# Second mixer on one Trainium2 core: differential output ahead of a weight unit, and first-layer weight units ahead of the norms

## Chip, cores and metric
The kernel runs on one core of a Trainium2 chip. The metric is the device time of one execution in microseconds; lower is better.

## The reference
Two blocks follow each other on an activation of 256 tokens by 1024 features, in float32, each with two layers. The second block's layer is, cut to what matters here:

```python
h = rms_norm_2(x, attn_norm)
proj = h @ w_in                     # 1024 x 5444
aq, ak, av, iq, ik, iw, bq, bk, bv, gates = split_cols(proj)
...                                 # head norms and rotary embedding
ya = sparse_attention(aq, ak, av, iq, ik, iw, k_sel)     # 64 best keys by index scores
yb = diff_attention(bq, bk, bv, lam)                     # p0 - lam * p1
yb = rms_norm_2(yb, b_subln) * (1.0 - lam_init)
g_a, g_b = sigmoid(gates + gate_bias)
x = x + (g_a * (ya @ w_up_a) + g_b * (yb @ w_up_b)) @ w_out
x = x + (silu(gate) * up) @ w_ffn_out                    # of rms_norm_2(x, ffn_norm)
```
The first block has other mixers and two feed-forward parts per layer, and ends with a norm, so that the second block's first layer works on a normed activation: its norm comes out of two sums of squares.

## The kernel before
Every float32 matmul by a weight is done as three: the weight is split into a high part (rounded) and a low part (the rest), and so is the activation, and high by high, high by low and low by high are added up (`three`, L1953). Weights come in units of 128 x 2048 elements, 1 MB, through four buffers. SP loads a unit into `raw`; ScalarE makes the high part (`split`, L709, busy at L717), VectorE the low part (`split`, L1215, busy at L1222), and TensorE consumes it (`split_ready`, L1959). Each engine has its own program, an order written out by hand, and they meet at semaphores. A unit can be split once the unit four before it is used.

A layer of the second mixer projects in 11 column tiles of two units each (`full_k`, L1979): positions 0 to 15 of a tile, one position being the three matmuls of one 128-row slice of the weights. Positions 0 to 3 and 8 to 11 are the first 128 tokens, the others the second. When a tile's first half is done (position 11, semaphore `tile_half`), the copy or gate of that half may begin. Beside the positions, functions `beside_bk` (tile 2) to `beside_g3` (tile 10) put the attention's small work: turns (transposes) of rotated heads (`turn`), index scores, then for each pair of heads scores (`pair_qk`), the turn of the probabilities (`pair_turn`), and the product with the values (`diff_pv`, `sparse_pv`). Pairs 0 to 3 belong to the differential attention, 4 to 7 to the sparse one.

What touches the change:

- **Start of a layer.** ScalarE turns the transposed activation into high parts with the gain (`stage`, L743), VectorE into low parts (L1245). Squares are summed on ScalarE (`square`, L719; in the first layer also `square_scaled`, L997), VectorE makes the mean (`norm`, or `two_norms`, L1232), ScalarE the root. ScalarE's copy of tile 0 (`evac(0)`, L1031) needs it. GpSimd then rotates the index heads and their key (`rotate2`, from L649), scales, copies (L686) and signals `rot_ready`, for which `rotated(0)` in `beside_bk` waits on TensorE, ahead of `turn((0, 1))`. Turned items are copied by ScalarE (`item(0)`) and VectorE (`item(1)`, L1355); item 5 is VectorE's last, and the first scores (`pair_qk(0)`, L2490) in tile 5 wait for it.
- **End of the projections.** At position 8 of tile 10 TensorE turns the differential output (L1965), ScalarE copies high parts (`diff_hi`, L1104), VectorE makes the low parts (`diff_lo`, L1796). At position 12 comes `pair_turn(7)` (L2505), which waits for `diff_lo`, since both use the same banks. VectorE's `gate(10, 0)` (L1703) needs tile 10's `tile_half`. `probs_turned(7)` copies the turned pair 7 on ScalarE (one half) and VectorE (the other, L1785); `sparse_pv(7)` (L2532) waits for both. It stands behind the first position of the up-projection, whose units are P2_UP to P2_UP + 3.

Of the kernel before, what the change touches and what calls it, by code (L numbers as in the profile page):

```python
# [56 lines left out]
P2_UP = P2_WIN + 2 * len(WIN2)  # L57
# [5 lines left out]
GAIN_FFN1, GAIN_MIX, GAIN_FFN2, GAIN_ATTN, GAIN_FFN, GAIN_FINAL = (2 * KC * k for k in range(6))  # L63
# [37 lines left out]
def stream1(l):  # L101
    return Stream(l * U1)
# [6 lines left out]
def build(nc, I, out):  # L109
    L = DEPTH  # L110
    with ExitStack() as ctx:
# [278 lines left out]
        PARTS = ((0, 0), (0, 1), (1, 0), (1, 1))  # L390
# [317 lines left out]
        def _(act):  # L708
            def split(st, p, it=0, m=None, c=4):  # L709
                s = st.slot(p)  # L710
                act.wait_ge(loaded[s], st.loads(p, it))

                act.wait_ge(units_used, st.freed(p, it))
                src, dst = raw[:, s, :], w_hi[:, s, :]
                if m is not None:
                    src, dst = (a.rearrange("p (c n) -> p c n", c=c)[:, :, 0:m] for a in (src, dst))
                nc.scalar.activation(dst, src, ACT.Copy).then_inc(units_hi, 1)  # L717

            def square(X, i, dump=xn, col=0):  # L719

                act.wait_ge(x_ready, X * 2 + (i + 1))
                nc.scalar.activation(dump[:, i, :], x[:, i, :], ACT.Square, accum_out=ss[:, col + i:col + i + 1])
# [20 lines left out]
            def stage(S, gain=None, parts=PARTS, first=0, banks=STAGE_BANKS):  # L743
                for n, (i, g) in enumerate(parts, first):
                    act.wait_ge(stage_T, S + (n + 1))
                    bank = ps[:, banks[2 * i + g], :].rearrange("p (c t) -> p c t", c=4)
                    tok = slice(P * i, P * i + P)
                    if gain is None:
                        o = nc.scalar.activation(aT_hi[:, 4 * g:4 * g + 4, tok], bank, ACT.Copy)
                    else:  # L750
                        for c in range(4):
                            o = nc.scalar.activation(aT_hi[:, 4 * g + c, tok], bank[:, c], ACT.Copy,
                                                     scale=gain_cols[:, gain + 4 * g + c:gain + 4 * g + c + 1])
                    o.then_inc(stage_hi, 1)
# [75 lines left out]
            for l in range(L):  # L830
                st = stream1(l)
# [37 lines left out]
                def exps(k):  # L869

                    for e in range(2):
                        act.wait_ge(pair_masked, (J + k) * 4 + (2 * e + 2))
                        for i, (c, n) in enumerate(((0, P), (P, 2 * P))):
                            nc.scalar.activation(pair_p[:, k % 2, e, c:c + n], pair_p[:, k % 2, e, c:c + n], ACT.Exp,
                                                 bias=pair_max[:, k % 2, e, i:i + 1], scale=-1.0,
                                                 accum_out=pair_sums[:, k % 2, e, i:i + 1])
                        nc.scalar.drain()
                        act.sem_inc(pair_exp, 1)
# [111 lines left out]
            for l in range(L):  # L990
                st = stream2(l)
                B = l * STAGES2 + STAGES1 * L
                N, W, T = l * 2 + 6, l * 11, l * TJ2 + TJ1 * L
                J, O = l * PAIRS2 + PAIRS1 * L, l * 2 + 4 * L
                if l == 0:

                    def square_scaled(i):  # L997
                        act.wait_ge(final_scaled, i + 1)
                        nc.scalar.drain()
                        nc.scalar.activation(junk[:, i, :], xn[:, i, :], ACT.Square, accum_out=ss[:, i:i + 1])  # L1000

                    junk = att[:, 0:2 * DM].rearrange("p (i n) -> p i n", i=2)
                    stage(B, GAIN_ATTN, PARTS[:2])
                    square(6, 0, junk, 2)
                    square_scaled(0)
                    stage(B, GAIN_ATTN, PARTS[2:], first=2)
                    split(st, 2)
                    square(6, 1, junk, 2)
                    square_scaled(1)
                    squared()  # L1010
                    root(N, 4)
                else:
                    stage(B, GAIN_ATTN + l * KC, PARTS[:2])
                    square(l * 2 + 7, 0)
                    split(st, 2)
                    stage(B, GAIN_ATTN + l * KC, PARTS[2:], first=2)
                    square(l * 2 + 7, 1)
                    squared()
                    root(N)
# [80 lines left out]
                def diff_hi():  # L1100

                    for i in range(2):
                        act.wait_ge(stage_T, B + (5 + i))
                        nc.scalar.activation(yb_hi[:, :, P * i:P * i + P],  # L1104
                                             ps[:, 6 + i, :].rearrange("p (c t) -> p c t", c=4), ACT.Copy)\
                            .then_inc(stage_hi, 1)
# [3 lines left out]
                        .then_inc(gates2_ready, 1)  # L1110

                evac(0)
                split(st, 3)
                head_squares(0)
                win_split(2, 0)
                head_roots(0)
# [68 lines left out]
                split(st, P2_UP)  # L1185
                probs_turned(6)
                exps(7)
                split(st, P2_UP + 1)
                diff_hi()
                split(st, P2_UP + 2)  # L1190
                probs_turned(7)
                act.wait_ge(tile_done, W + 9)
# [19 lines left out]
        def _(dve):  # L1212
            V = nc.vector

            def split(st, p, it=0, m=None, c=4):  # L1215
                s = st.slot(p)

                dve.wait_ge(units_hi, st.index(p, it) + 1)
                a, h, o = raw[:, s, :], w_hi[:, s, :].bitcast(F32), w_lo[:, s, :]
                if m is not None:  # L1220
                    a, h, o = (v.rearrange("p (c n) -> p c n", c=c)[:, :, 0:m] for v in (a, h, o))
                V.tensor_tensor(o, a, h, ALU.subtract).then_inc(units_split, 1)  # L1222
# [9 lines left out]
            def two_norms(N):  # L1232

                dve.wait_ge(squares, N + 1)
                V.tensor_scalar(ss[:, 2:4], ss[:, 2:4], 1.0 / DM, EPS, ALU.mult, ALU.add)
                V.tensor_scalar(ss[:, 0:2], ss[:, 0:2], 1.0 / DM, None, ALU.mult)
                V.drain()
                V.scalar_tensor_tensor(ss[:, 0:2], ss[:, 2:4], EPS, ss[:, 0:2], ALU.mult, ALU.add).then_inc(mean_sq, 1)  # L1240
                dve.wait_ge(roots, N + 1)
                V.reciprocal(rstd[:, 0:4], rstd[:, 0:4]).then_inc(rstd_ready, 1)
                V.drain()
# [172 lines left out]
            for l in range(L):  # L1416
                st = stream1(l)
# [248 lines left out]
            for l in range(L):  # L1666
                st = stream2(l)
                B = l * STAGES2 + STAGES1 * L
                N = l * 2 + 6
                if l == 0:  # L1670
                    stage(B, GAIN_ATTN, PARTS[2:], first=2)
                    split(st, 2)
                    two_norms(N)
                    split(st, 3)
                else:
                    stage(B, GAIN_ATTN + l * KC, PARTS[2:], first=2)
                    split(st, 2)
                    norm(N)
                    split(st, 3)
# [16 lines left out]
                def gate(n, i):  # L1696

                    c0, m = WIN2[n]
                    if i == 0:
                        dve.wait_ge(tile_half, l * 11 + (12 + n + 1))  # L1700
                    else:
                        dve.wait_ge(units_used, st.used(P2_WIN + 2 * n + 1))
                    V.scalar_tensor_tensor(proj2[:, i, c0:c0 + m], ps[:, BANK2[n][i], :], rstd[:, i:i + 1],  # L1703
                                           proj2[:, 1, c0:c0 + m], ALU.mult, ALU.add)\
                        .then_inc(tile_done if i else gate_first, 1)
                    V.drain()  # L1706
# [206 lines left out]
                probs_turned(6)  # L1913
                masked(7)
                probs(7)
                split(st, P2_UP + 1)
                diff_lo()
                gate(10, 0)
                split(st, P2_UP + 2)
                probs_turned(7)  # L1920
                gate(10, 1)
# [28 lines left out]
        def _(pe):  # L1950
# [18 lines left out]
            def stage(src, ready, n, i, banks=STAGE_BANKS):  # L1969

                pe.wait_ge(ready, n * 2 + (i + 1))
                turned(src, i, 0, banks)
                turned(src, i, 1, banks)
# [180 lines left out]
            for l in range(L):  # L2154
                st = stream1(l)
# [283 lines left out]
            for l in range(L):  # L2439
                st = stream2(l)  # L2440
                T, W, A, D = l * TJ2 + TJ1 * L, l * 11, l * 5 + 10, l * 5 + 12
                B, J, O = l * STAGES2 + STAGES1 * L, l * PAIRS2 + PAIRS1 * L, l * 2 + 4 * L
# [92 lines left out]
                    o.then_inc(pair_out, 1)  # L2535

                def beside_bk(at):
                    if at == 8:
                        rotated(0)
                        turn((0, 1))  # L2540
                    if at == 14:
                        copied(1, 1)
                        index_scores(0)

# [96 lines left out]
                first = second_half(x, x_ready, 6 if l == 0 else l * 2 + 7)  # L2641
# [107 lines left out]
```

## Time and profile before

| | |
|---|---|
| median of 3 runs | 1790.18 us (1790.01 to 1791.67) |
| profiled execution | 1789.88 us |
| its span in the profile | 1788.2 us |
| TensorE busy | 1774.5 us, 99% |
| VectorE busy | 1231.3 us, 69% |
| ScalarE busy | 987.8 us, 55% |
| GpSimd busy | 225.8 us, 13% |
| granted TensorE clock | 1.00 |
| HBM read | 313.94 MB, 176 GB/s |

PE is TensorE, PEld its weight loads, DVE VectorE, ACT ScalarE, POOL GpSimd. Busy time counts an instruction from its start to its modelled end, and TensorE's overlap: matmuls of 512 columns last 0.39 us each but follow one another every 0.227 us. Times of a timeline are counted from the start of the span.

### The profile page before, as it was taken

The numbers are of one execution on the slowest core, as the hardware profiler recorded it, in microseconds if no ns is written. First come the engines' busy times: TensorE is split into PE (matmuls) and PEld (weight loads), VectorE is DVE, ScalarE is ACT, GpSimd is POOL, SyncE is SP. The second block draws the span as 40 slices with busy tenths as digits, with TensorE's granted clock in tenths as the row PEclk, the third lists the DMA queues.
The fourth block names the chain that finished last, engine by engine and source line by source line (L and its number), as shares of the span: only waits on it lengthen the run. The fifth ranks groups of instructions, "written<-read, shape, count | busy, mean of one in ns | idle before, by whom it ended". The sixth has DMA issues, their size and how long they took to land.

```text
span 1788.2 us, 25450 instructions
## 1 busy us (share of the span) xinstructions
PE 1774.5 (99%) x9448; PEld 1479.0 (83%) x9448; DVE 1231.3 (69%) x1753; ACT 987.8 (55%) x1333; POOL 225.8 (13%) x255
## 2 busy tenths in 40 slices
PE   9999999999999999999999999999999999999999
PEld 8888877888888888877888877778888877788887
DVE  6775667677557755767676479966775599867763
ACT  6555585555445554666555376555554466645551
POOL 0000121000000000320000096200001383100000
PEclk9999999999999999999999999999999999999999
DMA  8656472555546564544565564545656544545551
GB/s 266 222 195 204 138 208 72 187 188 188 210 145 195 193 226 143 190 118 141 189 197 201 168 205 128 177 130 186 196 194 212 164 166 142 188 157 175 191 204 74
DMA packets 221517, 316.26 MB, mean 177 GB/s; under 512 B 14168, under 2 KB 162288, under 8 KB 221168
## 3 DMA queue, kind: packets, MB, share of 16 engines
q1 hardware_dynamic: 221392, 315.02, 53.9%
q8 instruction: 57, 0.93, 0.2%
q14 instruction: 36, 0.29, 0.0%
q10 hardware_dynamic: 32, 0.01, 0.0%
HBM read 313.94 MB, written 1.05 MB: 176 GB/s over the span
## 4 chain that ended last, share of the span: by engine, by line
PE 84%; DVE 10%; DVEq 3%; ACT 2%; issue 1%; ACTq 0%; POOLq 0%
PE ps L2091 25%; PE ps L1955 14%; PE ps L1957 13%; PE ps L1956 13%; PE ps L2092 13%; DVE w_lo L1222 3%; PE ps L1965 1%; PE ps L2179 1%; PE ps L2206 1%; PE ps L2194 1%; DVEq L1706 1%; ACT w_hi L717 1%; DVEq L1742 1%; DVE score L1731 1%; DVE att L1755 1%
## 5 line engine op out<-in xcount | busy, mean ns | idle before, releaser
L1222 DVE TENSOR_TENSOR w_lo<-raw,w_hi 128x2048 fp32r<-128x2048 f32 (+2 forms) x296 | 674.7, 2302 | 200.8 <-ACT w_hi L717 199.1
L2091 PE MATMUL ps<-aT,w_hi 128*128 128x512 f32 x1920 | 667.7, 392 | 0.0
L717 ACT ACTIVATE w_hi<-raw 128x2048 fp32r<-128x2048 f32 (+2 forms) x296 | 551.6, 1892 | 159.0 <-PE ps L1957 155.8
L2092 PE MATMUL ps<-aT,w_lo 128*128 128x256 f32 x1920 | 536.9, 280 | 0.0
L2091 PEld LDWEIGHTS ps<-aT,w_hi 128*128 128x128 f32 x1920 | 359.4, 187 | 80.4 <-issue 0.3
L2092 PEld LDWEIGHTS ps<-aT,w_lo 128*128 128x128 f32 x1920 | 362.5, 189 | 0.2
L1955 PE MATMUL ps<-w_hi,aT 128*128 128x512 f32 (+2 forms) x768 | 309.3, 403 | 4.3 <-DVE w_lo L1222 2.8
L1957 PE MATMUL ps<-w_hi,aT 128*128 128x512 f32 (+2 forms) x768 | 295.1, 384 | 0.0
L1956 PE MATMUL ps<-w_lo,aT 128*128 128x512 f32 (+2 forms) x768 | 294.3, 383 | 0.0
L1955 PE MATMUL ps<-w_hi,gT_hi 128*128 128x512 f32 x528 | 206.0, 390 | 0.0
L1957 PE MATMUL ps<-w_hi,gT_lo 128*128 128x512 f32 x528 | 205.6, 389 | 0.0
L1956 PE MATMUL ps<-w_lo,gT_hi 128*128 128x512 f32 x528 | 205.5, 389 | 0.0
L1955 PEld LDWEIGHTS ps<-w_hi,aT 128*128 128x128 f32 x768 | 144.3, 188 | 46.1 <-issue 16.7
L1957 PEld LDWEIGHTS ps<-w_hi,aT 128*128 128x128 f32 x768 | 144.2, 188 | 29.2
L1956 PEld LDWEIGHTS ps<-w_lo,aT 128*128 128x128 f32 x768 | 144.6, 188 | 22.9
L766 ACT ACTIVATE att<-ps 128x512 f32<-128x512 f32 x60 | 35.8, 597 | 162.2 <-PE ps L2092 162.2
L1957 PEld LDWEIGHTS ps<-w_hi,gT_lo 128*128 128x128 f32 x528 | 99.1, 188 | 20.7
L1956 PEld LDWEIGHTS ps<-w_lo,gT_hi 128*128 128x128 f32 x528 | 99.2, 188 | 20.4
L1955 PEld LDWEIGHTS ps<-w_hi,gT_hi 128*128 128x128 f32 x528 | 99.1, 188 | 20.4
L1313 DVE TENSOR_TENSOR att<-ps,att 128x512 f32<-128x512 f32 x60 | 41.5, 692 | 78.6 <-ACT att L771 78.6
L768 ACT ACTIVATE att<-att 128x512 f32<-128x512 f32 x60 | 37.9, 632 | 104.3 <-DVE att L1311 104.3
L618 POOL COPY tt<-proj 128x512 f32<-128x512 f32 x4 | 4.1, 1050 | 635.1 <-DVE proj L1453 635.1
(289 smaller groups left out, 1704.4 us busy)
## 6 DMA issues: line engine op xcount, KB each, us to landing
raw<-in_w_in SPq DMA_DIRECT2D x120, 512.0 KB, 4.5
raw<-in_w_ffn_down SPq DMA_DIRECT2D x88, 512.0 KB, 4.4
raw<-in_w_ffn_in SPq DMA_DIRECT2D x88, 512.0 KB, 5.0
raw<-in_w_ffn_gate SPq DMA_DIRECT2D x86, 512.0 KB, 4.2
raw<-in_w_ffn_up SPq DMA_DIRECT2D x86, 512.0 KB, 5.2
raw<-in_w_ffn_out SPq DMA_DIRECT2D x44, 512.0 KB, 4.8
raw<-in_w_out SPq DMA_DIRECT2D x32, 512.0 KB, 4.7
raw<-in_w_ck SPq DMA_DIRECT2D x8, 512.0 KB, 3.9
```

What stands on the lines that cost most here:

```text
L717: nc.scalar.activation(dst, src, ACT.Copy).then_inc(units_hi, 1)
L766: nc.scalar.activation(sil[:, b % 2], ps[:, bg:bg + 2, SEQ:2 * SEQ], ACT.Copy).then_inc(gate_lo, 1)
L768: nc.scalar.activation(sil[:, b % 2], sil[:, b % 2], ACT.Silu).then_inc(silu_done, 1)
L1222: V.tensor_tensor(o, a, h, ALU.subtract).then_inc(units_split, 1)
L1313: V.tensor_tensor(gg[:, b % 2], ps[:, bu:bu + 2, 0:SEQ], gg[:, b % 2], ALU.add)
L1706: V.drain()
L1731: V.scalar_tensor_tensor(score[:, c:c + n], relu[:, h % 2, c:c + n], iw[:, i, h:h + 1], (causal if h == 0 else score)[:, c:c + n], ALU.mul ...
L1955: M(o, ah, wh, start=start, stop=False)
L1956: M(o, ah, wl, start=False, stop=False)
L1957: return M(o, al, wh, start=False, stop=stop)
L2091: M(o, wh, aT[:, :, k, :], start=k == 0, stop=False, skip_group_check=True)
L2092: r = M(o[:, 0], wl, aT_hi[:, k, :], start=False, stop=k == KC - 1, skip_group_check=True)
```

## The change
Four orders change, and no instruction is added or removed.

- First layer: ScalarE splits unit 2 ahead of `stage` of the second 128 tokens and unit 3 right behind it, both ahead of `square_scaled(0)` and the squares that follow; its split of unit 3 behind `evac(0)` stays in the second layer alone. VectorE splits unit 3 ahead of `two_norms`.
- Both layers: `diff_hi` stands ahead of the split of unit P2_UP + 1 on ScalarE, and on VectorE that split stands behind `diff_lo` and `gate(10, 0)`.
- Both layers: in tile 2, `turn((0, 1))` goes from position 8 to 11, `index_scores(0)` from 14 to 15.

```diff
@@ ScalarE, first layer of the second mixer
                     square(6, 0, junk, 2)
+                    split(st, 2)
+                    stage(B, GAIN_ATTN, PARTS[2:], first=2)
+                    split(st, 3)
                     square_scaled(0)
-                    stage(B, GAIN_ATTN, PARTS[2:], first=2)
-                    split(st, 2)
                     square(6, 1, junk, 2)
@@
                 evac(0)
-                split(st, 3)
+                if l > 0:
+                    split(st, 3)
                 head_squares(0)
@@ ScalarE, both layers
                 exps(7)
+                diff_hi()
                 split(st, P2_UP + 1)
-                diff_hi()
                 split(st, P2_UP + 2)
@@ VectorE, first layer
                     split(st, 2)
+                    split(st, 3)
                     two_norms(N)
-                    split(st, 3)
@@ VectorE, both layers
                 probs(7)
-                split(st, P2_UP + 1)
                 diff_lo()
                 gate(10, 0)
+                split(st, P2_UP + 1)
                 split(st, P2_UP + 2)
                 probs_turned(7)
@@ TensorE, both layers
                 def beside_bk(at):
-                    if at == 8:
+                    if at == 11:
                         rotated(0)
                         turn((0, 1))
-                    if at == 14:
+                    if at == 15:
                         copied(1, 1)
                         index_scores(0)
```

## Rows read from the trace of the kernel before

**Rows 1.** The page's busy times: busy us, share of the span, instructions.
```profile
PE 1774.5 (99%) x9448; PEld 1479.0 (83%) x9448; DVE 1231.3 (69%) x1753; ACT 987.8 (55%) x1333; POOL 225.8 (13%) x255
```

**Rows 2.** TensorE's waits: total us, times, longest.
```profile
PE ps L1955 <- DVE w_lo L1222: 2.8, 4, 0.8
PE ps L2505 <- DVE yb_lo L1796: 2.0, 2, 1.1
```

**Rows 3.** TensorE's timeline, first layer, tiles 1 and 2: start, duration, [idle before].
```profile
1031.86 0.50 PE L1955 MATMUL ps<-w_hi,aT 128*128 128x512 f32 x1 [0.35 <-DVE w_lo L1222]
...
1038.36 0.50 PE L1955 MATMUL ps<-w_hi,aT 128*128 128x512 f32 x1 [0.73 <-DVE w_lo L1222]
...
1043.94 0.39 PE L1955 MATMUL ps<-w_hi,aT 128*128 128x512 f32 x1
```

**Rows 4.** ScalarE's and VectorE's timelines, start of the first layer.
```profile
1023.17 1.06 ACT L1000 ACTIVATE att<-xn 128x1024 f32<-128x1024 f32 x1
...
1025.29 2.17 ACT L752 ACTIVATE aT<-ps,gain_cols 128x128 fp32r<-128x128 f32 x8 [0.97 <-PE ps L1965]
...
1026.47 2.16 DVE L1255 SCALAR_TENSOR_TENSOR aT<-ps,gain_cols,aT 128x128 fp32r<-128x128 f32 x8 [0.60 <-ACT aT L752]
...
1029.30 2.50 DVE L1222 TENSOR_TENSOR w_lo<-raw,w_hi 128x2048 fp32r<-128x2048 f32 x1 [0.68 <-ACT w_hi L717]
...
1032.80 0.95 ACT L1031 ACTIVATE proj<-ps,rstd 128x324 f32<-128x324 f32 x2 [0.24 <-DVE rstd L1242]
```

**Rows 5.** Timelines of GpSimd and TensorE's weight loads up to the first turns, first layer.
```profile
1036.11 2.78 POOL L656 TENSOR_TENSOR proj<-proj,cs 128x256 f32<-128x256 f32 x1
...
1050.04 0.31 PEld L2137 LDWEIGHTS ps<-ident,proj 128*128 128x128 f32 x3 [0.24 <-POOLq L687]
```

**Rows 6.** Windows: us, busy per engine (instructions), clock, DMA; then VectorE's timeline there.
```profile
1043.90:1082.20 38.30, 38.30 (x186) 30.41 (x184) 32.24 (x32) 22.64 (x27) 36.21 (x27) 1.00 0.66 219
...
1050.95 0.43 DVE L1355 TENSOR_SCALAR tt<-ps 128x256 f32<-128x256 f32 x1 [1.94 <-PE ps L2137]
...
1054.31 3.18 DVE L1222 TENSOR_TENSOR w_lo<-raw,w_hi 128x2048 fp32r<-128x2048 f32 x1 [0.18 <-ACT w_hi L717]
```

**Rows 7.** Timelines of VectorE and TensorE at the first scores, first layer.
```profile
1081.46 0.68 DVE L1355 TENSOR_SCALAR tt<-ps 128x512 f32<-128x512 f32 x1
...
1082.24 0.93 PE L2490 MATMUL ps<-tt 64*128 64x128 f32 x8
```

**Rows 8.** The same places in the second layer: item 1, first scores.
```profile
1431.33 0.42 DVE L1355 TENSOR_SCALAR tt<-ps 128x256 f32<-128x256 f32 x1 [3.44 <-PE ps L2137]
...
1462.92 0.93 PE L2490 MATMUL ps<-tt 64*128 64x128 f32 x8 [0.16 <-issue]
```

**Rows 9.** Timelines of TensorE, ScalarE and VectorE around pair 7, first layer.
```profile
1164.87 1.03 PE L1965 MATMUL ps<-ident,xn 128*128 128x128 f32 x8
1165.73 1.07 ACT L1104 ACTIVATE yb_hi<-ps 128x512 fp32r<-128x512 f32 x2
1165.86 2.29 DVE L1222 TENSOR_TENSOR w_lo<-raw,w_hi 128x2048 fp32r<-128x2048 f32 x1 [0.79 <-ACT w_hi L717]
...
1167.80 0.39 PE L1955 MATMUL ps<-w_hi,aT 128*128 128x512 f32 x1
1168.06 1.28 DVE L1796 TENSOR_TENSOR yb_lo<-ps,yb_hi 128x512 fp32r<-128x512 f32 x2
1169.26 0.74 DVE L1703 SCALAR_TENSOR_TENSOR proj<-ps,rstd,proj 128x512 f32<-128x512 f32 x1
1169.49 0.85 PE L2505 MATMUL ps<-ident,att 128*128 128x128 f32 x6 [0.85 <-DVE yb_lo L1796]
...
1172.31 0.55 DVE L1785 COPY xn<-ps 128x384 f32<-128x384 f32 x1
...
1173.07 0.87 PE L2532 MATMUL ps<-xn,proj 128*64 128x256 f32 x8
```

**Rows 10.** TensorE's timeline at pair 7, second layer.
```profile
1550.45 0.84 PE L2505 MATMUL ps<-ident,att 128*128 128x128 f32 x6 [1.14 <-DVE yb_lo L1796]
```

## Prediction
> **What bounds the kernel now.** The profiled execution took 1789.88 us (span 1788.2, 1.68 around it), 0.30 under the median of 1790.18; the sum is made against 1789.88. About 0.2% (3.6 us) is what a measurement of this kernel can tell from no change. I read the page's busy shares first: TensorE is busy 99% of the span [rows 1], so only the 13.7 us in which it isn't can be gained. The waits of TensorE come next, for who ends these gaps: VectorE's weight splits and its low part of the differential output lead [rows 2]. Then the timelines around each moved line. Three things are to be seen there. First, both units of projection tile 1 come late in the first layer of the second mixer [rows 3]. Second, between 1043.9 and 1082.2 TensorE never rests, yet VectorE's queue is full as well, 32.24 of 38.30 us with GpSimd at 36.21 [rows 6]; its last link, the copy of item 5, ends at 1082.14, 0.1 before TensorE's first scores of the pair loop at 1082.24 [rows 7]. Third, the turn of pair 7 waits 0.85 and 1.14 us for the low part [rows 9, 10].
>
> **The start of the first layer.** Tile 1's first unit waits for a split that VectorE began at 1029.30, 0.68 idle, because ScalarE's half stood behind `stage` [rows 4]. Moved ahead, ScalarE's half fits where `square_scaled(0)` stood, from 1023.17 for 1.9 us to 1025.1, before `stage` begins at 1025.29: nothing is pushed. VectorE's stage ends at 1028.63, its split (2.50) at 1031.1; TensorE is free at about 1031.3, since its wait is 0.35 and the refill of its pipeline some 0.15 more. Unit 3 follows on VectorE at 1031.1 and is there at 1033.6, against a need at 1036.8: the wait of 0.73 goes, with its refill [rows 3]. TensorE's second half of tile 1, unwaited, took 5.58 and its first 6.50 [rows 3], so 0.9. Together **1.5 to 1.65 us, taken 1.6**, at the start of tile 2.
>
> The norms pay for it. VectorE's split ended at 1031.8 and the scaled copy (`evac(0)`) began at 1032.80: a chain of 1.0 [rows 4]. Behind both splits it starts at 1033.6, so the copy at 1034.6, 1.8 later. ScalarE's squares don't decide: its stage ends at 1027.5, unit 3's split (1.9) at 1029.4, and three squares of about 1.2 at 1033.0. Who waits: GpSimd's rotation (the copy feeds it), which in turn releases the first turns. SP's loads into the two buffers go out sooner, not later; none of these rows waits for a DMA.
>
> **The first turns, from position 8 to 11.** In the profile TensorE took them at 1050.04 to 1050.06 as GpSimd let them go [rows 5]. Three positions are 9 matmuls of 0.227 (a position is 0.68: eight of them are the 5.58 of a unit in rows 3, less the refill), 2.04 us. In the first layer TensorE comes there at 1050.06 - 1.6 + 2.04 = 1050.5. GpSimd starts 1.8 later, but of its 16.3 us from the copy's end (1033.75) to 1050.04 some are not work: one operation took 2.78 beside a split, against a mean of 1.34 over 27 [rows 5, 6], so up to 2 us each are waiting, and VectorE's splits (which stood behind the late unit 3) now come up to 2 us sooner and block one operation fewer. I get 1050.4, bounds 1049.9 (all the delay is made up) and 1051.8 (none). **The turns are 0.4 later** (bounds 0 and 1.9). In the second layer nothing is gained ahead, so they are **2.04 later**.
>
> That matters since ScalarE's item 0, its head squares, VectorE's sums and then the split of unit 7 queue behind the turns: VectorE idled 1.94 and 3.44 us for them [rows 6, 8], and from 1052.5 to item 5 it doesn't idle for TensorE again. Item 5 lets the scores go at 1082.24 and, in the second layer, 1462.92 (0.16 idle, refill more) [rows 7, 8]. What the queue loses up to there TensorE loses, whatever it had won: in the first layer the 1.6 are gone and 0.4 stands as a loss. In the second it would be 2.04. The unit split just behind the turns took 3.18 against 2.29 where GpSimd rests [rows 6, 9]; with GpSimd 2 us further ahead one of them falls in VectorE's idle time. I take **1.8 us** (bounds 0.9 and 2.1). Index scores at 15 instead of 14: 0.68 later at most, behind a queue that is later anyway, so nothing.
>
> The Trainium skill, SBUF — State Buffer (Reading the diagram), says that VectorE with two SBUF inputs and a reading GpSimd operation exclude each other for a whole instruction. The 2.78 and the 3.18 of this trace agree. Where the rule speaks for a smaller loss is a rival below.
>
> **The differential output ahead of unit P2_UP+1.** Before: VectorE splits from 1165.86, low parts 1168.06 to 1169.34, TensorE turns pair 7 at 1169.49; free it was at 1167.80 + 0.68 = 1168.48 [rows 9]. After: TensorE's transposes begin at 1164.87, the first four are done about 0.6 later, ScalarE's high parts (1.07 for both) end at 1166.6, VectorE's low parts at 1167.5. The wait goes, 1.0 us. But what is late next? `gate(10, 0)` now follows at once and needs tile 10's first half, whose last matmul ends at about 1168.65: VectorE, which used to split in this time, idles 1.2 us. Then 0.74 for the gate, 2.29 twice for the units UP+1 and UP+2, 0.55 for the copy of the turned pair 7 [rows 9]: 1168.7 + 0.1 + 0.74 + 4.5 + 0.5 = 1174.5. Before, that copy ended at 1172.86, and `sparse_pv(7)` began at 1173.07, just behind. It waits for it; now it begins at 1174.7, though TensorE is there at 1172.05. A wait of 2.6 stands in place of one of 1.0: **+1.6 us** (bounds 1.3 and 1.8). ScalarE ends its part of the turned pair at 1166.6 + 2 x 1.9 + 0.5 = 1170.9 and isn't the one waited for. Unit UP+1, split by 1171.8, is needed after `sparse_pv(7)` and the rest of unit UP, 21 matmuls of 0.227, at 1179 or later: hidden. SP's load into the buffer that this split frees goes out 3.7 us later (1171.8 for 1168.1); three units of 5.5 us still lie ahead of its use, so it costs nothing unless a load takes over 10 us. In the second layer the old wait was 1.14 instead of 0.85 [rows 10], so 0.3 less is lost: **+1.3** (1.0 and 1.6).
>
> **Sum.** 0.4 + 1.8 + 1.6 + 1.3 = 5.1; 1789.88 + 5.1 = **1795.0**. Ends: 0 + 0.9 + 1.3 + 1.0 = 3.2 and 1.9 + 2.1 + 1.8 + 1.6 = 7.4, so 1793.1 to 1797.3.
>
> **Rivals.**
> - *VectorE runs free of GpSimd behind the later turns* (not slower by more than 0.2%). The split behind them paid 0.9 over the free price [rows 6, 9]; if it and the next one run free, VectorE gets 1.8 back per layer: 0.4 - 1.8 = -1.4 and 2.0 - 1.8 = 0.2 at the first scores, with the ends' 2.9: +1.7, 1791.6. It decides once some 1.5 us in all are regained, which brings the sum of 5.1 to 3.6. For it: GpSimd gets 2 us of VectorE's idle time in the second layer. Against: it is busy 36.21 of 38.30 us and always has the next operation pending [rows 6]. By the rule of the Trainium skill, SBUF — State Buffer (Reading the diagram), this is the outcome if GpSimd runs out of work. Chance 0.12.
> - *GpSimd late at the turns.* One more operation blocked by a split, 2 us: turns at 1051.8 or beyond, 1.5 more: 6.6, 1796.5. Chance 0.12.
> - *Only the turn of pair 7 gains.* If something else than the copy held `sparse_pv(7)`, the ends bring -2.3, and with +2.2 ahead of them nothing is left: 1789.8. Against it stands the copy's end 0.2 before that matmul, and a plain queue. Chance 0.12.
> - *Every removed wait is gained* (faster): -1.6 - 1.0 - 1.3 = -3.9, 1786.0. It decides if VectorE's queue has 2 us to spare ahead of 1082 and 2.6 at pair 7; it shows no idle time there. Chance 0.06.
>
> **How the numbers follow.** My forecast has 0.58, and some 0.08 of it lies under 3.6 us. Slower 0.50 + 0.12 = 0.62 (rounded); within 0.2%: 0.08 + 0.12 + 0.12 and half of the last, 0.35; faster 0.03. The range leaves out the last two rivals and reaches from the first (1791.6, less 0.6 for runs and bounds) to the upper bound: 1791.0 to 1797.5.
>
> **What would show it.** The w_lo waits of tile 1 and the yb_lo waits gone; `evac(0)` of the first layer near 1034.6; turns at 1050.5 in the first layer and 2.04 later from the start of the layer in the second; item 5 on VectorE at 1081.9 in the first layer and, counted from the start of its layer, 1.8 later in the second, with a wait of TensorE of 2 us at or just behind the first scores in both; a new wait of 2.6 at `sparse_pv(7)` for the copy at L1785. If that wait is absent, the forecast is wrong by 3 to 5 us; if VectorE's item 5 isn't later, by about 2.

## The result, and the profile after

The changed kernel took 1795.46 us in the median of 10 runs (1793.33 to 1798.27), beside 1790.18 us of the kernel before (10 runs, 1789.75 to 1792.10) on the same chip: a ratio of 1.0025 [1.0017, 1.0033], 5.3 us slower. The profiled execution took 1795.33 us, with a span of 1793.6 and a granted clock of 1.00.

The page's span and busy times; they differ from [rows 1] by at most 0.7 us, so no engine has more work:

```profile
span 1793.6 us, 25450 instructions
PE 1774.9 (99%) x9448; PEld 1479.5 (82%) x9448; DVE 1232.0 (69%) x1753; ACT 987.8 (55%) x1333; POOL 226.3 (13%) x255
```

TensorE's waits after (total us, times, longest):

```profile
PE ps L2534 <- DVE xn L1787: 3.8, 2, 1.9
PE ps L2479 <- ACT xn L1066: 2.4, 2, 1.2
PE ps L1957 <- DVE w_lo L1224: 1.7, 2, 0.9
...
PE ps L2139 <- POOLq L666: 0.9, 2, 0.5
```

Against [rows 2], the two waits of tile 1's units and both waits of `pair_turn(7)` for `yb_lo` are gone. In their place stand two of 1.9 at `sparse_pv(7)` (L2534) for VectorE's copy of the turned pair, two of 1.2 at the second group of index scores (L2479), and two of 0.5 at the second turns.

TensorE's timeline where each second-mixer layer begins, before and then after. All times below are counted from these starts:

```profile
1022.90 0.31 PE L1955 MATMUL ps<-w_hi,aT 128*128 128x324 f32 x1
...
1404.73 0.31 PE L1955 MATMUL ps<-w_hi,aT 128*128 128x324 f32 x1
```
```profile
1024.90 0.31 PE L1957 MATMUL ps<-w_hi,aT 128*128 128x324 f32 x1
...
1407.75 0.31 PE L1957 MATMUL ps<-w_hi,aT 128*128 128x324 f32 x1
```

The mixer starts 2.0 us later after, though nothing ahead of it was changed; more on this under "What the hardware showed". From there:

| us from the layer's start | first turns | first scores | `pair_turn(7)` | `sparse_pv(7)` |
|---|---|---|---|---|
| first layer, before | 27.16 | 59.34 | 146.59 | 150.17 |
| first layer, after | 27.56 | 59.49 | 145.72 | 151.19 |
| second layer, before | 25.73 | 58.19 | 145.72 | 149.30 |
| second layer, after | 27.77 | 60.02 | 146.29 | 151.75 |

The first scores are 0.15 and 1.83 later, the stretch from there to `sparse_pv(7)` is 0.87 and 0.62 longer: 3.5 us in all. With the 2.0 of the start that is the span's difference, 1793.6 - 1788.2 = 5.4.

Start of the first layer after, timelines of VectorE and ScalarE, then of GpSimd, TensorE and VectorE up to the first scores:

```profile
1030.55 4.73 DVE L1224 TENSOR_TENSOR w_lo<-raw,w_hi 128x2048 fp32r<-128x2048 f32 x2
...
1036.29 0.95 ACT L1032 ACTIVATE proj<-ps,rstd 128x324 f32<-128x324 f32 x2 [0.25 <-DVE rstd L1244]
...
1051.38 0.40 POOL L686 COPY att<-proj 128x256 f32<-128x256 f32 x1
...
1052.46 0.60 PE L2139 MATMUL ps<-ident,proj 128*128 128x128 f32 x4
...
1053.31 0.42 DVE L1357 TENSOR_SCALAR tt<-ps 128x256 f32<-128x256 f32 x1 [4.75 <-PE ps L2139]
...
1060.32 0.93 PE L2479 MATMUL ps<-tt 64*128 64x128 f32 x8 [1.16 <-ACT xn L1066]
1066.69 1.09 PE L2139 MATMUL ps<-ident,proj 128*128 128x128 f32 x8 [0.45 <-POOLq L666]
...
1084.39 0.93 PE L2492 MATMUL ps<-tt 64*128 64x128 f32 x8
```

VectorE makes both units' low parts in one go, and the scaled copy of tile 0 starts 11.39 from the layer's start, 1.49 later than in [rows 4] (9.90). GpSimd's copy ends at 1051.78 (1051.38 + 0.40), and TensorE takes the turns at 1052.46 without a wait. VectorE idles 4.75 us ahead of item 1 where it had idled 1.94 [rows 6]. TensorE then stops twice within 14 us of the turns. In the second layer:

```profile
1435.52 0.60 PE L2139 MATMUL ps<-ident,proj 128*128 128x128 f32 x4
...
1436.38 0.42 DVE L1357 TENSOR_SCALAR tt<-ps 128x256 f32<-128x256 f32 x1 [5.46 <-PE ps L2139]
...
1467.77 0.93 PE L2492 MATMUL ps<-tt 64*128 64x128 f32 x8 [0.16 <-issue]
```

Here VectorE's idle time grew from 3.44 to 5.46 [rows 8], the 2.04 of three positions.

What leads from the first turns to TensorE's next stops can be read from GpSimd's rotation of the next heads. Its operation at L655 waits for ScalarE's squares of these heads (L1042, L1043 after), which stand in ScalarE's queue behind item 0, the copy of the first turns. That operation in the two layers, before and then after:

```profile
1052.80 1.29 POOL L655 TENSOR_TENSOR proj<-proj,rg 128x512 f32<-128x512 f32 x1
...
1433.17 1.30 POOL L655 TENSOR_TENSOR proj<-proj,rg 128x512 f32<-128x512 f32 x1
```
```profile
1054.91 1.29 POOL L655 TENSOR_TENSOR proj<-proj,rg 128x512 f32<-128x512 f32 x1 [0.42 <-ACT proj L1043]
...
1437.98 1.30 POOL L655 TENSOR_TENSOR proj<-proj,rg 128x512 f32<-128x512 f32 x1 [1.95 <-ACT proj L1043]
```

From the layer's start it begins at 29.90 and 28.44 before, at 30.01 and 30.23 after: 0.11 and 1.79 later. From there to TensorE's second turns 11.7 to 11.8 us pass in all four layers, and these turns come at 41.65 and 40.18 before, at 41.79 and 42.03 after: 0.14 and 1.85 later, as the first scores are. VectorE's item 5 ends 0.1 us ahead of the first scores in all four, and TensorE's idle time there (none, and 0.16) is the old one.

Pair 7 in the first layer after, to be laid beside [rows 9]:

```profile
1168.28 1.29 DVE L1798 TENSOR_TENSOR yb_lo<-ps,yb_hi 128x512 fp32r<-128x512 f32 x2 [1.05 <-ACT yb_hi L1105]
...
1169.94 0.39 PE L1957 MATMUL ps<-w_hi,aT 128*128 128x512 f32 x1
...
1170.14 0.75 DVE L1705 SCALAR_TENSOR_TENSOR proj<-ps,rstd,proj 128x512 f32<-128x512 f32 x1 [0.58 <-PE ps L1959]
1170.62 0.82 PE L2507 MATMUL ps<-ident,att 128*128 128x128 f32 x6
1170.98 4.50 DVE L1224 TENSOR_TENSOR w_lo<-raw,w_hi 128x2048 fp32r<-128x2048 f32 x2
1175.39 0.55 DVE L1787 COPY xn<-ps 128x384 f32<-128x384 f32 x1
1176.09 0.87 PE L2534 MATMUL ps<-xn,proj 128*64 128x256 f32 x8 [1.89 <-DVE xn L1787]
```

`pair_turn(7)` no longer waits. But two splits, 4.50 us, stand between the gate and the copy that `sparse_pv(7)` needs; before, one of them had already run.

### The profile page after: what moved, and what is told of

It reads as the page before. It is cut to its first block, busy times and chain, and to the rows that moved or that the text cites. A ratio compares the mean times of both kernels' runs of the same rounds, so it can differ in the third digit from the quotient of the medians.

```text
span 1793.6 us, 25450 instructions
## 1 busy us (share of the span) xinstructions
PE 1774.9 (99%) x9448; PEld 1479.5 (82%) x9448; DVE 1232.0 (69%) x1753; ACT 987.8 (55%) x1333; POOL 226.3 (13%) x255
## 4 chain that ended last, share of the span: by engine, by line
PE 87%; DVE 8%; DVEq 2%; ACT 1%; issue 1%; DMA 0%; ACTq 0%; POOL 0%; SPq 0%
PE ps L2093 25%; PE ps L1957 15%; PE ps L1959 14%; PE ps L1958 14%; PE ps L2094 13%; DVE w_lo L1224 2%; PE ps L1967 1%; PE ps L2208 1%; PE ps L2181 1%; PE ps L2196 1%; DVEq L1744 1%; DVE score L1746 1%; DVEq L1736 1%; DVE score L1733 1%; PE ps L2139 1%
```

## Experiments

The theory: turns at position 11 hold VectorE's and ScalarE's queues back by 1.8 us, which TensorE pays, in the first layer out of what the units ahead win; and at pair 7 the wait for `yb_lo` is traded for a longer one for the copy at L1787. The rivals: VectorE's queue is not what TensorE pays for, the moved units themselves cost something, or something other than the copy holds `sparse_pv(7)`. Edits below are to the kernel before unless said otherwise. One table for all. Two columns give by how much each layer's stretch from its start to `sparse_pv(7)` is longer than before's (150.17 and 149.30), in one profiled execution; then come the lowest of 10 to 12 runs less the lowest of the kernel before beside them, and the ratio of the runs with its interval.

| kernel | 1st layer | 2nd layer | sum | lowest run | ratio |
|---|---|---|---|---|---|
| the changed kernel | +1.02 | +2.45 | +3.5 | +3.6 | 1.0025 [1.0017, 1.0033] |
| e1, turns alone | +1.70 | +1.78 | +3.5 | +3.7 | 1.0019 [1.0010, 1.0027] |
| e2, pair 7 alone | +0.86 | +0.53 | +1.4 | +1.6 | 1.0010 [1.0002, 1.0019] |
| e3, first units alone | -0.18 | +0.04 | -0.1 | -0.1 | 0.9991 [0.9982, 0.9999] |
| e4, pair 7, copy first | +1.31 | -1.10 | | -1.7 | 0.9988 [0.9979, 0.9997] |
| e5, changed + copy first | -0.66 | +0.74 | +0.1 | -0.1 | 0.9996 [0.9987, 1.0005] |
| e6, changed, 2nd layer's turns at 8 | +0.93 | +0.61 | +1.5 | +1.6 | 1.0013 [1.0004, 1.0022] |
| e7, e3 and e4 together | -0.97 | -1.07 | -2.0 | -2.1 | 0.9993 [0.9984, 1.0002] |
| e7 again | -0.99 | -1.12 | -2.1 | -2.1 | 0.9986 [0.9977, 0.9995] |
| e8 | -0.85 | -0.94 | -1.8 | -1.8 | 0.9988 [0.9979, 0.9997] |
| e9 | -1.23 | -1.37 | -2.6 | -2.6 | 0.9985 [0.9976, 0.9994] |

The sum of the two stretches, from a single execution, agrees with the lowest run of each kernel to 0.2 us (e4's profile holds a disturbance, told there, and has no sum). So what these edits do lies in the two stretches. The medians scatter by 2 us around this, for two causes that stand under "What the hardware showed".

**e1: the later turns alone.**
```diff
                 def beside_bk(at):
-                    if at == 8:
+                    if at == 11:
                         rotated(0)
                         turn((0, 1))
-                    if at == 14:
+                    if at == 15:
```


> The kernel before with the one edit in beside_bk: first turns at position 11, first index scores at 15, both layers. My theory: VectorE's queue starts behind the turns and has no slack up to item 5, so TensorE loses what the turns lose less some 0.2: about 1.8 us in each layer, +3.6 in all, seen as item 5 and the first pair's scores 1.8 later, counted from the layer's start. Rival (VectorE makes it up, free of GpSimd): under 1 us in all. Second rival (later turns cost nothing by themselves, it was GpSimd's late start): 0.

Measured: median 1795.19 us, 1.0019 [1.0010, 1.0027]. The first scores come at 61.08 and 59.98, 1.74 and 1.79 later, and the rest is as before. TensorE's waits:

```profile
PE ps L1955 <- DVE w_lo L1222: 2.8, 4, 0.8
...
PE ps L2137 <- POOLq L666: 2.8, 2, 1.4
PE ps L2505 <- DVE yb_lo L1796: 2.0, 2, 1.2
```

The old waits of [rows 2] all stand; new is the wait of 1.4 in each layer at the second turns (`turn((2, 3))`, in tile 3) for GpSimd, plus one of 0.2 at the index scores. GpSimd's operation at L655, which ran without a wait before, here idles 1.88 us for ScalarE's squares in the first layer and 1.93 in the second. So later turns cost 1.8 us in each layer, and TensorE pays them at what ScalarE and GpSimd make for it, ahead of item 5. In the changed kernel's profile the same loss is split otherwise (1.2 at the index scores, 0.5 at the turns) and comes to the same; e5, whose orders are the changed kernel's up to pair 7, splits it as e1 does.

**e2: pair 7 alone.**
```diff
 ScalarE
+                diff_hi()
                 split(st, P2_UP + 1)
-                diff_hi()
 VectorE
-                split(st, P2_UP + 1)
                 diff_lo()
                 gate(10, 0)
+                split(st, P2_UP + 1)
                 split(st, P2_UP + 2)
                 probs_turned(7)
```


> The kernel before with diff_hi and diff_lo ahead of the split of unit P2_UP+1 on ScalarE and VectorE, as in the change, and nothing else. My theory: the waits of pair_turn(7) go (0.85 and 1.14), a wait of about 1.9 for VectorE's copy of the turned pair appears at sparse_pv(7) in both layers, net +0.9 and +0.6, +1.5 us. Rival (the wait's removal is the whole effect): -2.3 us. Rival (my first sum, a gate that waits 0.7 longer): +2.9.

Measured: median 1793.98 us, 1.0010 [1.0002, 1.0019]. Its wait in the first layer:

```profile
1175.73 0.87 PE L2532 MATMUL ps<-xn,proj 128*64 128x256 f32 x8 [1.89 <-DVE xn L1785]
```

`pair_turn(7)` comes 1.02 and 1.36 earlier, `sparse_pv(7)` 0.86 and 0.53 later: the changed kernel's two terms, without its other parts. The wait is the copy's, not something else's, and it is larger than the one removed.

**e3: the first layer's units alone.**
```diff
 ScalarE, first layer
+                    split(st, 2)
+                    stage(B, GAIN_ATTN, PARTS[2:], first=2)
+                    split(st, 3)
                     square_scaled(0)
-                    stage(B, GAIN_ATTN, PARTS[2:], first=2)
-                    split(st, 2)
...
-                split(st, 3)
+                if l > 0:
+                    split(st, 3)
 VectorE, first layer
                     split(st, 2)
+                    split(st, 3)
                     two_norms(N)
-                    split(st, 3)
```


> The kernel before with units 2 and 3 split ahead of the norms in the first layer, and the turns left at position 8, the pair 7 order left as it was. My theory: both waits of tile 1 go (0.35 and 0.73), TensorE comes to the turns 1.6 us earlier and waits there for GpSimd, which is ready at about the old time: a wait of 1.3 to 1.5 us at the turns, then everything as before: -0.2 us, between -0.4 and +0.3. Rival (the gained 1.6 us stay gained): -1.6.

Measured: median 1789.96 us, 0.9991 [0.9982, 0.9999]; the first scores are 0.16 earlier. Waits:

```profile
PE ps L1957 <- DVE w_lo L1224: 1.7, 2, 0.8
...
PE ps L2139 <- POOLq L687: 1.3, 1, 1.3
```

The interval lies under 1 because of the kernel before: 19 of its 35 runs beside e3 are above 1791 us, and one of e3's 11 (for the causes under "What the hardware showed"). The lowest runs and the stretches differ by 0.1. The waits at tile 1 go, as wanted, and one of 1.3 comes at the first turns, whose GpSimd work starts later. The units ahead are harmless and gain nothing by themselves: GpSimd, not the units, sets when the first turns can be. In the changed kernel this wait is absent because the turns have been moved behind it, and the queues pay.

**e4: pair 7, with the copy ahead of the second split.** ScalarE as in e2; VectorE:
```diff
-                split(st, P2_UP + 1)
                 diff_lo()
+                split(st, P2_UP + 1)
                 gate(10, 0)
-                split(st, P2_UP + 2)
                 probs_turned(7)
+                split(st, P2_UP + 2)
```


> The kernel before with diff_hi ahead of the split on ScalarE, and on VectorE the order diff_lo, split of P2_UP+1, gate(10, 0), copy of the turned pair 7, split of P2_UP+2. My theory: VectorE's copy is done at about 1171.1 in the time of before, before TensorE comes to sparse_pv(7) at 1172.05, so both waits are gone in both layers: -2.3 us. Rival (the copy isn't what sparse_pv(7) waits for in the changed kernel, or a later wait takes the gain): 0 or more.

Measured: median 1789.92 us, 0.9988 [0.9979, 0.9997]; the second layer's stretch is 1.10 shorter. In the first layer of the profiled execution VectorE's split for tile 1 took 4.44 us instead of 2.50 [rows 4]:

```profile
1029.43 4.44 DVE L1222 TENSOR_TENSOR w_lo<-raw,w_hi 128x2048 fp32r<-128x2048 f32 x1 [0.68 <-ACT w_hi L717]
...
1033.93 0.80 PE L1955 MATMUL ps<-w_hi,aT 128*128 128x512 f32 x1 [2.29 <-DVE w_lo L1222]
```

That is ahead of anything the kernel changes. From the first scores to `sparse_pv(7)`, behind it, 89.98 us stand against 90.83 before, 0.85 shorter. So most of the two old waits for `yb_lo` can be gained once only one split stands between the low part and the copy: e2 lost 1.4 us and e4 gains 2.0 (0.85 + 1.10) where 2.3 were expected, with a wait of 0.2 left at `sparse_pv(7)`. Against e2 two moves were made together: the split of P2_UP + 1 goes ahead of the gate as well. No run has them apart. By the changed kernel's durations the gate first, then one split and the copy would end at about 1173.7 (1170.14 + 0.75 + 2.29 + 0.55), ahead of 1174.20, when TensorE comes to `sparse_pv(7)`. By this estimate the copy's place ahead of the second split would be enough.

**e5: the changed kernel with that order on VectorE.**
```diff
                 diff_lo()
-                gate(10, 0)
                 split(st, P2_UP + 1)
-                split(st, P2_UP + 2)
+                gate(10, 0)
                 probs_turned(7)
+                split(st, P2_UP + 2)
```


> The changed kernel with VectorE's order at pair 7 mended: diff_lo, split of P2_UP+1, gate(10, 0), copy of the turned pair 7, split of P2_UP+2. My theory (sizes from the sections of the profiles so far): the layers cost +0.15 and +1.83 at the first scores and bring 0.9 and 1.1 at pair 7, so the profile stands within 0.3 us of the kernel before with no wait at sparse_pv(7). And the granted clock: I hold that its falls in the changed kernel come behind the waits of 1.9 us at sparse_pv(7), so without them no run should show a clock under 1.00 more often than runs of the kernel before do. Rival (the falls come from something else in the change): clocks of 0.999 and 0.998 in half of the runs, as in the changed kernel.

Measured: median 1789.80 us, 0.9996 [0.9987, 1.0005]. Pair 7 in the first layer:

```profile
1170.62 2.29 DVE L1224 TENSOR_TENSOR w_lo<-raw,w_hi 128x2048 fp32r<-128x2048 f32 x1 [1.00 <-ACT w_hi L717]
1172.84 0.74 DVE L1705 SCALAR_TENSOR_TENSOR proj<-ps,rstd,proj 128x512 f32<-128x512 f32 x1
1173.74 0.56 DVE L1787 COPY xn<-ps 128x384 f32<-128x384 f32 x1 [0.17 <-issue]
```

`sparse_pv(7)` waits 0.19 instead of 1.89, and 3.4 us of the changed kernel's 3.5 are back (1.02 + 0.66 and 2.45 - 0.74). What is left of the loss is the second layer's turns, hidden here by the two gains. On the clock: none of its 11 runs shows one under 1.00, against 3 of 33 of the kernel before beside it, so the rival (half of the runs) fails.

**e6: the changed kernel, in the second layer with the turns at 8 and 14.**
```diff
-                    if at == 11:
+                    if at == (11, 8)[l]:
...
-                    if at == 15:
+                    if at == (15, 14)[l]:
```


> The changed kernel with the first turns at position 8 and the index scores at 14 again in the second layer alone. My theory: the first scores of the second layer come 58.2 us after the layer's start instead of 60.0, 1.8 less for the whole kernel, so +1.65 against before in the profile; first layer unchanged at 59.5. Rival (VectorE's other work sets item 5, not the turns): no difference, +3.5.

Measured: median 1793.47 us, 1.0013 [1.0004, 1.0022]. The second layer's first scores come at 58.21, as before (58.19), and its stretch is longer by pair 7's 0.61 alone. The turns' 1.8 in the second layer is thus measured from both sides, by putting them in (e1) and by taking them out.

**e7: units ahead and copy first, turns left at 8** (e3 and e4 together).

> The kernel before with units 2 and 3 ahead of the norms in the first layer, turns at 8 in both layers, and at pair 7 the mended order (copy ahead of the split of P2_UP+2). My theory: -0.2 at the first scores of the first layer, 0 in the second, -0.9 and -1.1 at pair 7: -2.2 us, faster than both kernels. Rival (the parts aren't additive, e.g. a wait for a later up unit takes the gain): 0.

And for the second time:

> e7 unchanged, for a comparison on one chip with the version above: -2.1 us against before in the lowest run and in the sections of the profile. If its median again stands within 0.5 us of before while its lowest run is 2 us under it, the runs fall into two groups some 2 us apart that the change doesn't make.

Measured: median 1789.71 us, 0.9993 [0.9984, 1.0002], and, run again beside e9, 1787.94, 0.9986 [0.9977, 0.9995]. Both executions give the same stretches to 0.05 us. The second median doesn't stand within 0.5 us of before, but 2.3 under it (1790.26): 9 of the 11 runs were in the lower of two groups, where it had been 5 of 11. Of its waits, one of 1.3 stands at the first turns, as in e3. Parts that don't touch each other add up: -0.1 of e3 and -2.0 of e4, against -2.0 and -2.1 measured. It leaves the 1.3 at the first turns.

**e8: e5, with unit 7 split ahead of the turned items.** This asks whether VectorE's idle time ahead of the late turns can be used.
```diff
 ScalarE
                 evac(1)
+                win_split(3, 1)
                 item(0)
                 head_squares(1)
-                win_split(3, 1)
                 head_roots(1)
 VectorE
+                win_split(3, 1)
                 item(1)
                 head_sums(1)
-                win_split(3, 1)
                 head_scales(1)
```


> The changed kernel with the mended order at pair 7, and with the split of tile 3's second unit ahead of item 0 on ScalarE and of item 1 on VectorE, in both layers, so that it fills the time in which both wait for the later turns. My theory: VectorE's queue behind the turns is shorter by one split (2.3 to 3.2 us), so it isn't the bound at item 5; GpSimd's rotation is blocked by the split for up to 2 us, and TensorE waits for it at the turns by up to 2 us in the first layer and about 0 in the second. Net at the first scores: about -0.5 to +0.5 in the first layer, 0 to -0.5 in the second, then up to 1 us more per layer as the later waits for VectorE (0.3, 0.5, 0.8) shrink; with the pair 7 gain some -3 us. Rival (VectorE's queue isn't what binds at the first scores): item 5 comes no sooner than in the changed kernel, total near 0.

Measured: median 1788.20 us, 0.9988 [0.9979, 0.9997]. VectorE's timeline:

```profile
1058.34 2.72 DVE L1224 TENSOR_TENSOR w_lo<-raw,w_hi 128x2048 fp32r<-128x2048 f32 x1 [1.55 <-ACT w_hi L717]
1060.98 1.78 DVE L1733 SCALAR_TENSOR_TENSOR score<-xn,iw,causal 128x128 f32<-128x128 f32 x2
...
1081.76 0.68 DVE L1357 TENSOR_SCALAR tt<-ps 128x512 f32<-128x512 f32 x1
```

The second layer's first scores come at 58.36, 1.65 earlier than in e5 (60.01): the late turns cost almost nothing once work stands ahead of them. In the first layer they come only 0.13 earlier, since TensorE waits 1.3 at the first turns (28.96). In place of the full queue there is now an idle stretch of 1.55 for ScalarE's half of tile 4's first unit. In that stretch GpSimd's operation at L658 has no split beside it. Second layer, e5 and then e8:

```profile
1439.06 3.14 POOL L658 TENSOR_TENSOR proj<-proj 128x512 f32<-128x512 f32 x1
```
```profile
1437.36 1.28 POOL L658 TENSOR_TENSOR proj<-proj 128x512 f32<-128x512 f32 x1
```

The rotation starts no sooner (L655 at 30.48, in e5 at 30.24), but takes 1.86 less there, and the second turns come at 40.41 for 41.99, without the wait of 1.4 for GpSimd. VectorE's score operations are 1.65 sooner too, as expected; but the wait that TensorE lost was the one for GpSimd. The whole gain was 1.8 us where some 3 were expected.

**e9: e8, with ScalarE's split of that unit ahead of its roots.**
```diff
                 head_squares(1)
+                win_split(4, 0)
                 head_roots(1)
-                win_split(4, 0)
```


> As e8, and on ScalarE the split of tile 4's first unit ahead of the root of the second head norm, both layers: in e8 VectorE idled 1.55 us for that split, 3.3 us after the turns, which gave back what the moved unit 7 had won. My theory (VectorE's queue from the turns to the ninth tile is one chain, and TensorE's later waits of 0.3, 0.5, 0.3 and 0.8 us hang on it): item 5 comes about 1.8 us sooner than in e8 in both layers, the first scores 0.3 to 0.5 sooner, the later waits shrink, 3 us less than e8 in all, lowest run near 1785. Rival (the later waits hang on other work, or TensorE's own pace is the bound at the first scores and nothing behind it moves): 0 to -0.8 against e8.

Measured: median 1787.61 us, 0.9985 [0.9976, 0.9994].

```profile
1058.36 2.88 DVE L1224 TENSOR_TENSOR w_lo<-raw,w_hi 128x2048 fp32r<-128x2048 f32 x1
1061.16 2.81 DVE L1733 SCALAR_TENSOR_TENSOR score<-xn,iw,causal 128x128 f32<-128x128 f32 x2
...
1082.97 0.68 DVE L1357 TENSOR_SCALAR tt<-ps 128x512 f32<-128x512 f32 x1
```

The idle stretch is gone and VectorE's split begins 1.59 earlier from the layer's start (33.52 for 35.11; the starts are 1024.84 and 1023.23), but item 5 comes only 0.40 earlier. Of the 1.43 with which the next pair of operations starts ahead, 1.03 is lost in it (2.81 for 1.78). That is a miss: an idle gap in a queue is not worth its length here. The whole gain against e8 is 0.8 us in the stretches and in the lowest run, where 3 were expected; it is the rival's figure. e9 is the best of the kernels tried and beats both; against e7 in the same runs it is 0.3 us in the median and 0.5 in the stretches, too little to call.

## Why the prediction was right, and where not

The direction, and 1795.0 against a median of 1795.46, came out, though not by the sum's own terms: these were 5.1 and measured 3.5. That the total is so near is luck.

- **First scores, first layer:** 0.4 forecast, 0.15 measured. The turns came at 27.56, just 0.4 later than before. Right in that what tile 1 wins the first turns lose (e3); of the 0.4, GpSimd's rotation at L655 took over only 0.11. The scaled copy came 1.49 later and not 1.8.
- **First scores, second layer:** 1.8 forecast, 1.83 measured, 1.79 in e1, 1.8 in e6. The size was right, the path was not: I looked for a wait at or just behind the first scores, and in the first layer it stood 24 and 18 us ahead of them (1060.32 and 1066.69, against 1084.39), in the second 24 and 18 as well, at the index scores and the second turns. The second turns wait for GpSimd's rotation, and that for ScalarE's squares behind item 0; VectorE's sums aren't in this chain. The index scores wait for a copy of ScalarE, whose root before it had waited 0.86 for those sums. I followed VectorE's queue alone. That queue is late by as much (its score operations begin 38.19 us from the second layer's start, before 36.35), so what it would cost TensorE by itself isn't separated; but the wait ahead of the first scores didn't grow. And the 0.2 that I took off the three positions' 2.04 fits another cause: in the second layer before, the squares were done at 1432.86, 0.3 ahead of L655 (1433.17), and that slack is used up first.
- **Pair 7:** 1.6 and 1.3 forecast, 0.87 and 0.62 measured. This is the step that was mis-sized, by 0.7 in each layer: the start of `gate(10, 0)`, and with it the new wait at `sparse_pv(7)`. The mechanism held (e2 shows it alone, e4 and e5 undo it): the new wait was 1.89 and not 2.6. I let tile 10's first half end just before `pair_turn(7)`, at 1168.65 of before. But `tile_half` is signalled at position 11 and `pair_turn(7)` stands behind the matmuls of position 12, which [rows 9] show at 1167.80, a position before the turn. So the gate could begin 0.68 sooner: after, it starts 0.48 ahead of `pair_turn(7)` (1170.14, 1170.62). All that follows on VectorE (0.75, 4.50, 0.55) was as costed.
- **The rest,** 5.4 - 3.5 in the profiled execution, is the later start of the mixer (below). It is in the median too: the two middle runs, 1795.33 and 1795.60, show a clock of 1.00, and five others with falls of the clock reach up to 1798.27. No step forecast either, and by luck their size made up for the error at pair 7.

Of the rivals: "VectorE free of GpSimd" fails, the second layer loses 1.83 and not 0.2; "GpSimd late at the turns" fails, the turns came when forecast; "only the turn of pair 7 gains" fails at the copy's wait; "every removed wait is gained" fails too: with another order most of it is gained at pair 7 (e4), but at the start e3 gains 0.1.

## What to carry over

A removed wait is worth what the next thing in the same queue leaves of it. Ahead of moving an operation, write down who waits for the *end* of the queue behind it; moving a weight split of 2.3 us behind a small urgent copy instead of ahead of it turned, together with the gate's move behind the first split, a loss of 1.4 us into a gain of 2.0. Follow every queue that the moved operation releases: here the price of the later turns came through ScalarE's squares and GpSimd's rotation, and not at the end of VectorE's queue. And where one engine lies on the path 99% of the time, compare sections of the trace from a common matmul on: here the two of a kernel added up to the difference of its lowest run within 0.2 us, while medians of 11 runs of one kernel, on two chips, lay 1.8 apart.

## What the hardware showed

**The clock falls behind a single wait of 1.9 us, in part of the executions.** Windows behind `sparse_pv(7)` of the first layer in e2, with its neighbours, then of the kernel before (columns: window, its length, busy time and instructions of PE, PEld, DVE, ACT, POOL, granted clock, DMA share, GB/s):

```profile
1175.00:1177.00 2.00, 1.27 (x10) 0.99 (x11) 1.25 (x3) 2.00 (x2) 0.00 (x0) 1.00 0.97 375
1177.00:1181.00 4.00, 4.00 (x13) 3.12 (x12) 2.89 (x2) 2.66 (x3) 0.00 (x0) 0.57 0.72 279
1181.00:1182.00 1.00, 1.00 (x6) 0.83 (x5) 0.00 (x0) 0.00 (x0) 0.00 (x0) 1.00 0.42 57
...
1560.00:1562.00 2.00, 2.00 (x6) 1.52 (x6) 1.06 (x2) 2.00 (x3) 0.00 (x0) 0.50 1.07 352
```
```profile
1177.00:1181.00 4.00, 4.00 (x19) 3.24 (x18) 3.26 (x3) 2.75 (x2) 0.00 (x0) 1.00 0.29 60
```

TensorE has the new wait from 1173.84 to 1175.73. In the window from 1177 to 1181 the mean granted clock is 0.57, most of it at 0.50 (1.2 GHz in place of 2.4), and 13 matmuls run where before has 19; then it is 1.00 again. In the second layer, behind the same wait, the clock is 0.50 from 1560 to 1562 as well. The two layers of e2 start 384.25 us apart, against 381.83 before; with the 0.86 of pair 7 taken off, the fall costs 1.56. 8 of e2's 12 runs and 5 of the changed kernel's 10 show a mean clock under 1.00 (0.999 to 0.997), but only 2 of the 11 of e6, which has both waits too and ran on another chip than e2. None of the 77 runs of e1, e3, e5, e7 (twice), e8 and e9 does, which lack this wait. The kernel before has such runs, 13 of 88, and e4 2 of 11. e4's profile shows one: its wait of 2.29 at tile 1 ends at 1033.93, and right behind it the clock is 0.50:

```profile
1034.00:1036.00 2.00, 2.00 (x5) 1.63 (x6) 0.36 (x3) 1.45 (x4) 0.22 (x1) 0.50 0.47 88
```

No profile of the kernel before holds a fall, so that its falls come from such a wait is not shown. A forecast of a wait that is near 2 us has to carry this cost on top; here it is up to 3.1 us for two waits, more than pair 7's own 1.5. What decides whether an execution falls was not tested.

**Two groups of runs, 2 us apart.** Most kernels have runs in two groups at a clock of 1.00 (before: 1789.65 to 1790.61 and 1791.56 to 1792.47, with three of 75 runs at 1793.5 to 1794.1). In the profiles the second mixer then begins at 1022.9 to 1023.3 or at 1024.7 to 1024.9, whatever the kernel. The difference arises in the first feed-forward part. Lines of the window from 36 to 60 us, before and after (form and count, busy, mean ns, idle ahead):

```profile
L2091 PE MATMUL ps<-aT,w_hi 128*128 128x512 f32 x70 | 24.3, 394 | 0.0
```
```profile
L2093 PE MATMUL ps<-aT,w_hi 128*128 128x512 f32 x69 | 24.4, 399 | 0.0
```

TensorE never rests there, yet a matmul takes 1% longer. Laid beside before matmul by matmul, the changed kernel is 0.1 us late at 31 us of the span, 1.9 at 126 and 2.0 from 146 on. The program is the same in this stretch; the cause is open. With e7's lowest runs 0.1 apart and 5 and 9 of 11 runs in the lower group, this accounts for its two medians, 1.8 us apart.

**GpSimd takes back what VectorE gains.** In e9 operations that start 1.4 us sooner end 0.4 sooner; beside GpSimd, the split on VectorE takes 2.88 and the pair of score operations 2.81, against 2.72 and 1.78 in e8. In the window 1055 to 1083 GpSimd is busy 26.79 of 28.00 us in e8 and in e9 alike, so there is nearly always an operation ready to fall on VectorE's. In e9:

```profile
1055.00:1083.00 28.00, 28.00 (x139) 22.38 (x138) 25.31 (x28) 16.08 (x20) 26.79 (x18) 1.00 0.41 134
```

The Trainium skill, SBUF — State Buffer (Reading the diagram), says that whichever of the two starts first holds the shared ports for its whole instruction; these durations are in accord with it. The other side of it shows at GpSimd's L658: 3.14 us beside a split (e5), 1.28 where VectorE idles (e8). No run here took GpSimd's work away.
